# Expert results added to the tokens by one-hot products between the next pair's matrix products

## The chip, the cores and the metric

The kernel runs on one core of a Trainium2 chip. The metric is the device time of one execution in microseconds (us); lower is better. TensorE is called PE, VectorE DVE, ScalarE ACT, GpSimd POOL and SyncE SP, as in the profile.

## What is computed

Two transformer-like blocks over 512 tokens of width 1024, all in float32. The first (attention, recurrent branch, dense MLP) and the mixer of the second are not touched by the change. The change is in the last stage, a mixture of 64 experts of which each token uses two:

```python
y_pad = lax.map(expert_block, (x_pad..., block_e))   # silu(x@w_gate)*(x@w_up) @ w_down, per expert
y = y_pad[dest] * w_s[:, None]                       # weight of each of the 1024 (token, expert) rows
out = jax.ops.segment_sum(y, tok_s, num_segments=t)  # two rows to each token
```

`x + out` is then normalised and written. Each expert has three matrices of 2 MB (1024x512, 1024x512, 512x1024), so the stage reads 64 x 3 x 2 MB = 402.6 MB of weights, each once.

## The kernel before

The kernel has one hand-ordered program for each engine; semaphores carry the dependences. Experts are worked on two at a time, 32 pairs (`PAIRS`). Each expert has 64 places for tokens (`CAP`), so a pair's rows fill the 128 partitions; its two experts' products use 64 columns of the PE array each, side by side. (Tokens beyond 64 of one expert would go through the loop `more_rounds`, which these inputs do not enter.)

For pair q PE issues, in `pe_pair`: 8 transposes of the gathered token rows XG (tiles "xt", L992); gate and up products "g" and "u" (L1008, 8 k-steps x 2 experts each, N=512); 4 transposes of the activations ("at", L1015); the down products "d" in two halves (L1040; the last pair has its own order, L1028, that follows the weights as they land). A float32 product is two MATMUL records in the trace, so g and u are 64 records, d is 32. A tile is one of 8 PSUM banks, taken in turn by `any_bank`; `open_tile` waits until the bank's former tile was read.

Around it: DVE scales xt into XT (L2184), DVE and ACT turn g and u into AT (tanh L1423, DVE L2189 and L2194), ACT copies the transposes to aT (L1427), and DVE (L2204) and ACT (L1433) copy the halves of d into YE, the pair's 128 result rows. For pairs 0 to 30 POOL then scatters YE to a DRAM tensor `y_d` (L2321), a row for each (token, choice); the writers of YE wait for this of the pair before (`y_st`). POOL also gathers the token rows of pair q+2 into XG (L2317), queued behind the scatter of pair q-1 and ahead of that of pair q.

At the end eight gathers (L2317, `YA`, semaphores comb0 to comb7) fetch `y_d` back by token, and DVE adds each to X with its weight (`dve_comb`, L2126, eight instructions of 128x1024). Only pair 31 goes another way, `pe_spread` (L982): YE is scaled by the row's weight (`WTAB`, a small product "wtab", L961, behind pair 0), and multiplied by four one-hot matrices OH (128 rows x 128 tokens, made by `dve_hots`, L2140), one for each block of 128 tokens: 8 products of K=128, M=128, N=512, that is 16 records. `dve_spread` (L2133) adds these eight PSUM tiles to X. Then `act_end` (L1440, squares of each block), `dve_end` (root, L2210) and `sync_end` (output).

SP loads the weights, 192 loads of 2 MB into a ring of nine buffers (`RING`). Load n waits for the end of the products that used load n-9: each of g, u and d releases two buffers.

The lines of the writers of YE and of the PE loop:

```python
            if q:
                act.wait_ge(S("y_st"), 16 * q)                                   # L1430
...
                pe_pair(pe, T, q, ..., any_bank, ("gather", q % 2, 16 * ((q + 1) // 2)))   # L956
                if q == 0:                                                       # wtab, L957 to L962
...
            pe_spread(pe, PAIRS - 1, any_bank)                                   # L965
```

Of the kernel before, what the change touches and what calls it, by code (L numbers as in the profile page):

```python
# [16 lines left out]
PAIRS = 32  # L17
ENDS = 31
WIDE = 30
NONE = 4096  # L20
# [128 lines left out]
def program(nc, A, out):  # L149
    with ExitStack() as ctx:  # L150
# [160 lines left out]
        OK, o2 = zl(2, 4), zl(2, 4)  # L311
        V, WA, BW = zl(2, 4), zl(2, 4), zl(8, PAIRS - WIDE)
        GY = zl(2, 4).bitcast(I32)
        WTAB, TOKF = zl(PAIRS - WIDE), zl(PAIRS - WIDE)
        SLOTS, BM, BM0 = zl(128), zl(2, 4, 32), zl(2, 4)
# [18 lines left out]
        done_ck = SB[:, 4096 + CK_COLS["neg"][0]:4096 + CK_N + SM_N + 8 * 72 + 72 + 400]  # L334
        OH = [view(zone, 4096 + 512 * n, 4, 128) for n in range(3)]
        YA = [view(done_ck, 0, 1024), view(done_ck, 1024, 1024), view(zone, xt0 + 1024, 1024), row]
        YA += [view(EXTRA[0], 1024 * n, 1024) for n in range(4)]
        row2 = EXTRA[4][:, 0:1024]
# [24 lines left out]
        def slot(*name):  # L363
            return SLOT[W.at[name][0]]
# [12 lines left out]
        def tensor_program(pe):  # L377
# [575 lines left out]


            for q in range(PAIRS):
                pe_pair(pe, T, q, lambda n: loaded("ex", 6 * q + n), lambda n: slot("ex", 6 * q + n), any_bank, ("gather", q % 2, 16 * ((q + 1) // 2)))  # L956
                if q == 0:  # L957
                    o = open_tile(pe, ("wtab",), any_bank())
                    pe.wait_ge(S("bw"), 1)
                    for n in range(8):  # L960
                        ins = pe.matmul(o[:, 0:PAIRS - WIDE], AM[:, n // 4, n % 4, :], BW[:, n, :], start=n == 0, stop=n == 7)  # L961
                    ins.then_inc(T.f("wtab"), 1)  # L962
                for n in range(6):
                    W.ended[("ex", 6 * q + n)] = (("g", q), ("g", q), ("u", q), ("u", q), ("d", q, 1), ("d", q, 1))[n]
            pe_spread(pe, PAIRS - 1, any_bank)  # L965
            pe.wait_ge(S("rounds"), 1)

# [6 lines left out]

        def pe_spread(pe, q, bank):
            pe.wait_ge(S("oh"), 4)
            pe.wait_ge(*T.free("d", q, 0))
            pe.wait_ge(*T.free("d", q, 1))
            for i in range(4):
                for nh in range(2):  # L980
                    o = open_tile(pe, ("sp", q, i, nh), bank())
                    pe.matmul(o, OH[q - WIDE][:, i, :], YE[:, 512 * nh:512 * nh + 512], start=True, stop=True).then_inc(T.f("sp", q, i, nh), 1)  # L982

        def pe_pair(pe, table, q, ready, weight, bank, gathered):
            x = XT
# [8 lines left out]
            for mat, name in enumerate(("g", "u")):  # L994
                o = open_tile(pe, (name, q), bank(), 1, table)
                parts = mat == 1 and q == PAIRS - 1
                if not parts:
                    pe.wait_ge(*ready(2 * mat))
                    pe.wait_ge(*ready(2 * mat + 1))
                for k in range(8):  # L1000
                    if mat == 0 and k % 4 == 0:
                        pe.wait_ge(*table.free("xt", q, k // 4))
                    if parts and k == 0:
                        pe.wait_ge(S("up0"), 16)
                    if parts and k % 4 == 0:
                        pe.wait_ge(S(f"up{1 + k // 4}"), 16)
                    for e in range(2):
                        ins = pe.matmul(o[64 * e:64 * e + 64, :], x[:, k, 64 * e:64 * e + 64],  # L1008
                                        weight(2 * mat + e)[:, 512 * k:512 * k + 512], start=k == 0, stop=k == 7)
                ins.then_inc(table.f(name, q), 1)  # L1010
            o = open_tile(pe, ("at", q), bank(), 1, table)
            pe.wait_ge(*table.free("u", q))
            a = AT.rearrange("p (a b) -> p b a", b=4)
            for k in range(4):
                ins = pe.transpose(o[:, 128 * k:128 * k + 128], a[:, k, :], ident)  # L1015
            ins.then_inc(table.f("at", q), 1)
            pe.wait_ge(*table.free("at", q))
            if q == PAIRS - 1:
# [400 lines left out]
        def act_pair(act, table, q):  # L1419
# [9 lines left out]
            if q:  # L1429
                act.wait_ge(S("y_st"), 16 * q)  # L1430
            if q == ENDS:
                act.wait_ge(*table.free("wtab"))
            act.activation(YE[:, 512:1024], table.ap("d", q, 1), ACT.Copy,  # L1433
                           scale=WTAB[:, q - WIDE:q - WIDE + 1] if q >= ENDS else 1.0).then_inc(table.s("d", q, 1), 1)

# [11 lines left out]
        def vector_program(dve):  # L1447
# [623 lines left out]
            def weights():  # L2071
# [19 lines left out]
                flat8 = HI.rearrange("p a b -> p (a b)")  # L2091
                after(tt(BW, bc(iota[:, WIDE:PAIRS], 1, 8), bc(flat8, 2, PAIRS - WIDE), ALU.is_equal))
                dve.tensor_tensor(BW, BW, bc(WT.rearrange("p a b -> p (a b)"), 2, PAIRS - WIDE), ALU.mult).then_inc(S("bw"), 1)
                dve_rows(dve, own, ENDS)


            for q in range(ENDS):
                dve_pair(dve, T, q, weights if q == 0 else None)
                if q == 0:
                    copy(("wtab",), WTAB, T.ap("wtab")[:, 0:PAIRS - WIDE])  # L2100
                if q == 2:
                    dve_hots(dve, own)
            q = PAIRS - 1
            dve_xt(dve, T, q)
            dve_gate(dve, T, q)
            dve_up(dve, T, q)
            for i in range(2):
                dve_tokens(dve, i)
            dve_ye(dve, T, q)
            dve_tokens(dve, 2)  # L2110
            for i in range(2):
                dve_spread(dve, q, i)
            dve_tokens(dve, 3)
            for i in range(2, 4):
                dve_spread(dve, q, i)

        def dve_tokens(dve, i):
            for n in (2 * i, 2 * i + 1):
                dve_comb(dve, n, S("comb"), YA[n], S(f"comb{n}"))

# [6 lines left out]

        def dve_spread(dve, q, i):
            dve.wait_ge(S("comb"), 2 * i + 2)
            for nh in range(2):  # L2130
                xs = X[:, i, 512 * nh:512 * nh + 512]
                dve.wait_ge(*T.full("sp", q, i, nh))
                dve.tensor_tensor(xs, xs, T.ap("sp", q, i, nh), ALU.add).then_inc(S("xadd"), 1)  # L2133

        def dve_hots(dve, own):
            dve.wait_ge(*T.free("tab"))
            dve.wait_ge(own.sem, own(dve.tensor_copy(TOKF, TAB[:, WIDE:PAIRS])))
            for p in range(1, 2):
                for i in range(4):
                    dve.tensor_scalar(OH[p][:, i, :], ck("iota"), TOKF[:, p:p + 1], -128.0 * i, ALU.subtract, ALU.is_equal).then_inc(S("oh"), 1)  # L2140
        def dve_plan(dve, own, table):
# [28 lines left out]

        def dve_pair(dve, table, q, between=None):
            dve_xt(dve, table, q)
            if between:
                between()
            dve_gate(dve, table, q)
            dve_up(dve, table, q)
            dve_ye(dve, table, q)

# [17 lines left out]
        def dve_ye(dve, table, q):  # L2196
            dve.wait_ge(*table.full("d", q, 0))
            if q:
                dve.wait_ge(S("y_st"), 16 * q)
            if q >= ENDS:  # L2200
                dve.wait_ge(*table.free("wtab"))
                dve.tensor_scalar(YE[:, 0:512], table.ap("d", q, 0), WTAB[:, q - WIDE:q - WIDE + 1], None, ALU.mult).then_inc(table.s("d", q, 0), 1)
            else:
                dve.tensor_copy(YE[:, 0:512], table.ap("d", q, 0)).then_inc(table.s("d", q, 0), 1)  # L2204
# [25 lines left out]
        def gpsimd_program(pool):  # L2230
# [66 lines left out]
            for q in range(1, 3):  # L2297
                gather(pool, XG[q % 2], hn_d, TAB[:, q:q + 1], 511, S(f"gather{q % 2}"))
            for q in range(ENDS):
                if 0 < q < PAIRS - 2:  # L2300
                    pool.wait_ge(*T.full("xt", q, 1))
                    gather(pool, XG[q % 2], hn_d, TAB[:, q + 2:q + 3], 511, S(f"gather{q % 2}"))
                pool.wait_ge(*T.free("d", q, 0))
                pool.wait_ge(*T.free("d", q, 1))
                scatter(pool, DEST[:, q:q + 1], S("y_st"))


            pool.wait_ge(S("y_st"), 16 * ENDS)
            pool.wait_ge(S("gy"), 1)
            for n in range(8):  # L2310
                if n == 4:
                    pool.wait_ge(*T.full("u", PAIRS - 2))
                gather(pool, YA[n], y_d, GY[:, n % 2, n // 2:n // 2 + 1], 1023, S(f"comb{n}"))
            pool.wait_ge(S("xadd"), 8)
# [411 lines left out]
```

## Time and profile before

| what | us |
|---|---|
| median of three runs | 2460.68 (2452.25 to 2461.19) |
| the profiled execution | 2447.28 |
| its span, first to last instruction | 2445.4 |
| expert stage: first g product to last d product | 1469.3 to 2424.2 |
| rest: last pair's spread, sums, norm, output | 2424.2 to 2445.4 |

The profiled execution's own time lies 1.9 us above its span. Times in views count from the start of the span. A slice of the page's picture is 61 us; a digit is the busy share in tenths. In a timeline row the columns are start, duration, engine, line, operation, output and inputs, shapes, count, and in brackets the idle time of that engine just before and what ended it. "MATMUL ... 128*64" is an instruction on 64 columns of the array, "128*128" on all. The granted clock is 1.00 for 2.4 GHz and 0.5 for 1.2 GHz.

### The profile page before, as it was taken

To read this page: it belongs to the slowest core of one execution; us is meant where nothing else is said; L and a number is where in the kernel's file an instruction comes from. 1 tells how busy PE (TensorE), PEld (TensorE's weight loads), DVE (VectorE), ACT (ScalarE), POOL (GpSimd) and SP (SyncE) were. 2 spreads that over 40 slices of the span, in tenths; PEclk is the share of its full clock that TensorE was granted. 3 is DMA by queue.
4 is the path that set the end of the run, shared out by engine and by line. 5 is a ranking of instruction groups with operands and counts; after the bars stand their busy time and mean duration, and the time that the engine had idled before them with its cause. 6 is when DMAs were issued, how large, how long until landed. Compare 5 with 4: busy or idle time off the path is not lost.

```text
span 2445.4 us, 20383 instructions
## 1 busy us (share of the span) xinstructions
PE 2226.5 (91%) x8284; PEld 1022.6 (42%) x8284; DVE 612.2 (25%) x1311; ACT 323.1 (13%) x652; POOL 206.8 (8%) x186
## 2 busy tenths in 40 slices
PE   8999999999999999999999999988888888877886
PEld 4554444445444444466644463333323333322332
DVE  2246544311633210033431142111111111111114
ACT  2014424202111100021110120000000000000001
POOL 0001111010344200000000001000000000000001
PEclk9999999999999999998999999998999999999998
DMA  6201010322232321219422339999999999999995
GB/s 273 86 35 69 35 69 4 151 103 78 95 118 79 141 77 72 101 52 161 155 102 83 159 156 408 426 426 426 425 426 426 426 427 427 425 425 422 421 426 221
DMA packets 69759, 552.43 MB, mean 226 GB/s; under 512 B 21656, under 2 KB 26392, under 8 KB 37600
## 3 DMA queue, kind: packets, MB, share of 16 engines
q1 hardware_dynamic: 42384, 515.49, 51.8%
q10 hardware_dynamic: 17200, 23.23, 3.2%
q0 software_dynamic: 10080, 12.38, 1.4%
q8 instruction: 67, 1.10, 0.2%
q14 instruction: 28, 0.23, 0.0%
HBM read 543.91 MB, written 35.68 MB: 237 GB/s over the span
## 4 chain that ended last, share of the span: by engine, by line
PE 69%; DMA 26%; DVE 3%; ACT 1%; issue 1%; DVEq 0%; POOL 0%; SPq 0%; ACTq 0%; POOLq 0%
PE ps L380 25%; DMA sb<-in_eu 12%; PE ps L1008 9%; PE ps L456 8%; DMA sb<-in_eg 8%; PE ps L698 8%; PE ps L1040 4%; DMA sb<-in_ed 4%; PE ps L399 2%; PE ps L856 2%; PE ps L628 2%; PE ps L541 1%; PE ps L574 1%; PE ps L568 1%; DMA sb<-in_mgg 1%
## 5 line engine op out<-in xcount | busy, mean ns | idle before, releaser
L380 PE MATMUL ps<-sb 128*128 128x512 f32 (+2 forms) x1536 | 613.8, 559 | 2.8 <-issue 1.4
L1008 PE MATMUL ps<-sb 128*64 128x512 f32 x2048 | 487.7, 632 | 108.6 <-DMA sb<-in_eu 79.3
L380 PEld LDWEIGHTS ps<-sb 128*128 128x128 f32 x1536 | 279.7, 190 | 315.9 <-issue 312.6
L1008 PEld LDWEIGHTS ps<-sb 128*64 128x64 f32 x2048 | 176.7, 145 | 398.8 <-issue 398.7
L1040 PE MATMUL ps<-sb 128*64 128x512 f32 x992 | 232.5, 623 | 26.9 <-ACT sb L1427 17.2
L456 PE MATMUL ps<-sb 128*128 128x512 f32 x512 | 236.1, 600 | 0.3 <-DMA sb<-in_mgg 0.3
L698 PE MATMUL ps<-sb 128*128 128x512 f32 x448 | 192.5, 592 | 0.7 <-ACT sb L1247 0.7
L1451 DVE TENSOR_TENSOR sb<-sb 128x32 f32<-128x32 f32 (+10 forms) x292 | 115.4, 412 | 115.7 <-PE ps L662 66.2
L1040 PEld LDWEIGHTS ps<-sb 128*64 128x64 f32 x992 | 73.7, 143 | 164.2 <-issue 137.6
L456 PEld LDWEIGHTS ps<-sb 128*128 128x128 f32 x512 | 91.3, 190 | 100.0 <-issue 98.9
L698 PEld LDWEIGHTS ps<-sb 128*128 128x128 f32 x448 | 85.0, 190 | 107.6 <-issue 107.6
L2321 POOL DMA_INDIRECT y_d<-sb x31 | 31.2, 1007 | 853.1 <-PE ps L992 745.8
L2194 DVE SCALAR_TENSOR_TENSOR sb<-sb,ps 128x512 f32<-128x512 f32 x32 | 22.1, 690 | 300.8 <-PE ps L1008 294.2
L1070 ACT ACTIVATE sb<-ps 128x512 f32<-128x512 f32 (+4 forms) x103 | 54.6, 538 | 252.6 <-PE ps L380 90.9
L2189 DVE SCALAR_TENSOR_TENSOR sb<-sb,ps 128x512 f32<-128x512 f32 x32 | 22.1, 690 | 242.3 <-ACT sb L1423 242.3
L1475 DVE COPY sb<-ps 128x512 f32<-128x512 f32 (+6 forms) x53 | 34.5, 651 | 160.9 <-PE ps L380 89.8
L2239 POOL TENSOR_TENSOR sb<-sb 128x256 f32<-128x256 f32 (+3 forms) x32 | 41.6, 1300 | 377.4 <-DVE sb L1669 377.3
L1427 ACT ACTIVATE sb<-ps 128x512 f32<-128x512 f32 x32 | 19.1, 598 | 375.0 <-PE ps L1015 375.0
L2184 DVE TENSOR_TENSOR sb<-ps,sb 128x512 f32<-128x512 f32 x64 | 41.4, 688 | 101.8 <-PE ps L992 101.1
L2204 DVE COPY sb<-ps 128x512 f32<-128x512 f32 x31 | 21.5, 693 | 181.2 <-PE ps L1040 181.2
L399 PE MATMUL ps<-sb 128*128 128x256 f32 x256 | 59.6, 393 | 6.5 <-DVE sb L1470 3.5
L856 PE MATMUL ps<-sb 128*128 128x512 f32 x128 | 58.4, 598 | 1.6 <-DVE sb L1985 1.6
(283 smaller groups left out, 1481.5 us busy)
## 6 DMA issues: line engine op xcount, KB each, us to landing
sb<-in_eg SPq DMA_DIRECT2D x64, 2048.0 KB, 33.6
sb<-in_eu SPq DMA_DIRECT2D x63, 2048.0 KB, 33.9
sb<-in_ed SPq DMA_DIRECT2D x63, 2048.0 KB, 32.4
sb<-in_m SPq DMA_DIRECT2D x16, 2048.0 KB, 7.4
sb<-in_mg SPq DMA_DIRECT2D x8, 1536.0 KB, 6.9
sb<-in_winF SPq DMA_DIRECT2D x5, 2048.0 KB, 7.3
sb<-in_mgg SPq DMA_DIRECT2D x4, 2048.0 KB, 8.0
sb<-in_wo SPq DMA_DIRECT2D x4, 2048.0 KB, 7.3
```

The source lines that it names most:

```text
L380: ins = pe.matmul(out, lhsT, rhs, start=k == 0, stop=k == len(pieces) - 1)
L399: ins = pe.matmul(T.ap(*tile)[:, t], lhsT, rhs[:, t], start=k == 0, stop=k == 7)
L456: ins = pe.matmul(o, lhsT, rhs, start=k == 0, stop=k == 7)
L628: ins = pe.matmul(o, MG1[:, k, 128 * i:128 * i + 128], wo[nh][:, k, :], start=k == 0, stop=k == 7)
L698: ins = pe.matmul(acc[2 * i + nh], HT[:, k, 128 * i:128 * i + 128], w[:, q, 512 * nh:512 * nh + 512], start=k == 0, stop=False)
L856: ins = pe.matmul(T.ap(*name), MG2[:, k, 128 * i:128 * i + 128], wo[nh][:, k, :], start=k == 0, stop=k == 7)
L1008: ins = pe.matmul(o[64 * e:64 * e + 64, :], x[:, k, 64 * e:64 * e + 64], weight(2 * mat + e)[:, 512 * k:512 * k + 512], start=k == 0, stop ...
L1040: ins = pe.matmul(o[64 * e:64 * e + 64, :], aT[:, k, 64 * e:64 * e + 64], weight(4 + e)[:, d:d + 512], start=k == 0, stop=k == 3)
L1070: act.activation(dst, T.ap(*name) if src is None else src, ACT.Copy).then_inc(T.s(*name), 1)
L1451: return own(dve.tensor_tensor(o, a, b, op))
L2184: dve.tensor_tensor(XT[:, 4 * hf:4 * hf + 4, :], table.ap("xt", q, hf).rearrange("p (a b) -> p a b", a=4), bc(ck("gx")[:, 4 * hf:4 * hf + ...
L2239: pool.tensor_tensor(pr, pr, bc(ST[u % 4][:, 2:4], 2, nk), ALU.mult).then_inc(S("prob"), 1)
```

## The change

Every pair's result goes to the tokens by the way that only pair 31 had. The scatters, the eight gathers, `dve_comb` in the main path and the wait `y_st` are removed. All YE are scaled by the row's weight as they are copied (WTAB now has 32 columns). The products of pair q-1's YE with its one-hot matrices are issued inside pair q, in three places: the blocks 0 and 1 (4 products) between g and u, block 2 (2 products) between u and at, block 3 between at and d. Pair 31's come after it, as before. The writers of YE wait for the last of these products of the pair before. DVE makes four one-hot matrices for each pair and adds eight PSUM tiles to X for each. In pair 0 the product "wtab" moves from behind d to between u and at. POOL only gathers XG.

```diff
             for q in range(PAIRS):
-                pe_pair(...)
-                if q == 0:
-                    ... wtab ...
+                def meanwhile(place):
+                    if q:
+                        pe_spread(pe, q - 1, any_bank, ((0, 1), (2,), (3,))[place])
+                    elif place == 1:
+                        weight_table()
+                pe_pair(..., meanwhile)
-            pe_spread(pe, PAIRS - 1, any_bank)
+            pe_spread(pe, PAIRS - 1, any_bank, range(4))
...
+        def pe_spread(pe, q, bank, blocks):
+            if 0 in blocks:
+                pe.wait_ge(S("oh"), 4 * q + 4)
+                pe.wait_ge(*T.free("d", q, 0))
+                pe.wait_ge(*T.free("d", q, 1))
+            for i in blocks:
                 for nh in range(2):
                     o = open_tile(pe, ("sp", q, i, nh), bank())
+                    pe.matmul(o, OH[q % 2][:, i, :], YE[:, 512 * nh:512 * nh + 512], start=True, stop=True)...
...
                 ins.then_inc(table.f(name, q), 1)      # end of g (mat 0) and of u (mat 1)
+                if meanwhile:
+                    meanwhile(mat)
...
             ins.then_inc(table.f("at", q), 1)
+            if meanwhile:
+                meanwhile(2)
             pe.wait_ge(*table.free("at", q))
...
             if q:
-                act.wait_ge(S("y_st"), 16 * q)
+                act.wait_ge(*table.full("sp", q - 1, 3, 1))
...
+            for q in range(PAIRS):
+                def meanwhile(place):
+                    if q:
+                        dve_spread(dve, q - 1, ((0, 1), (2, 3))[place])
+                    if place == 0:
+                        if q == 0:
+                            weights()
+                            ... TOKF from TAB ...
+                        dve_hots(dve, q)
+                    elif q == 0:
+                        copy(("wtab",), WTAB, ...)
+                dve_pair(dve, T, q, meanwhile)
+            dve_spread(dve, PAIRS - 1, range(4))
...
             dve_gate(dve, table, q)
+            if meanwhile and q:
+                meanwhile(0)
             dve_up(dve, table, q)
+            if meanwhile:
+                meanwhile(1)
             dve_ye(dve, table, q)
...
-                pool.wait_ge(*T.free("d", q, 0))
-                pool.wait_ge(*T.free("d", q, 1))
-                scatter(pool, DEST[:, q:q + 1], S("y_st"))
-            pool.wait_ge(S("y_st"), 16 * ENDS)
-            pool.wait_ge(S("gy"), 1)
-            for n in range(8):
-                ...
-                gather(pool, YA[n], y_d, GY[:, n % 2, n // 2:n // 2 + 1], 1023, S(f"comb{n}"))
```

## Rows read from the trace of the kernel before

**Rows 1.** The page, part 2: busy tenths in 40 slices of 61 us.
```profile
PE   8999999999999999999999999988888888877886
...
DMA  6201010322232321219422339999999999999995
```

**Rows 2.** Windows: stretch, length, busy us (instructions) by engine, clock, DMA share, GB/s.
```profile
1547.53:1572.46 24.93, 22.79 (x109) 9.04 (x109) 3.37 (x6) 1.79 (x3) 2.03 (x3) 1.00 1.00 424
1944.03:1974.72 30.69, 24.70 (x109) 9.40 (x109) 3.36 (x5) 1.79 (x3) 2.02 (x2) 0.94 1.01 427
```

**Rows 3.** The chain that ended last, late in the expert stage: start, us, what.
```profile
2383.17 32.17 DMA sb<-in_ed
```

**Rows 4.** DMA queues, 1900 to 2200 us: packets, MB, share of 16 engines.
```profile
q1 hardware_dynamic: 8575, 124.92, 98.0%
q0 software_dynamic: 2880, 2.68, 2.6%
```

**Rows 5.** Timeline of pair 3, in which PE waits for no weights.
```profile
1547.53 13.96 PE L1008 MATMUL ps<-sb 128*64 128x512 f32 x64 [0.51 <-DVE sb L2184]
...
1562.43 0.72 PE L1015 MATMUL ps<-sb 128*128 128x128 f32 x4 [0.94 <-DVE sb L2194]
...
1563.84 7.09 PE L1040 MATMUL ps<-sb 128*64 128x512 f32 x32 [0.69 <-ACT sb L1427]
...
1572.46 13.95 PE L1008 MATMUL ps<-sb 128*64 128x512 f32 x64 [0.51 <-DVE sb L2184]
```

**Rows 6.** Timeline of a pair in mid-stage: the up products.
```profile
1944.03 8.78 PE L1008 MATMUL ps<-sb 128*64 128x512 f32 x32 [3.34 <-DMA sb<-in_eu]
...
1974.72 8.78 PE L1008 MATMUL ps<-sb 128*64 128x512 f32 x32 [3.40 <-DMA sb<-in_eu]
```

**Rows 7.** Timelines of single PE records where the tile shape changes.
```profile
1517.92 1.03 PE L1040 MATMUL ps<-sb 128*64 128x512 f32 x4
...
1518.77 0.60 PE L1040 MATMUL ps<-sb 128*64 128x512 f32 x2
1519.30 0.44 PE L992 MATMUL ps<-sb 128*128 128x128 f32 x2
...
1468.83 0.50 PE L950 MATMUL ps<-sb 128*128 128x64 f32 x3
1469.26 0.65 PE L1008 MATMUL ps<-sb 128*64 128x512 f32 x2
```

**Rows 8.** Timelines of single PE records: first and last of the spread products.
```profile
2425.15 0.67 PE L982 MATMUL ps<-sb 128*128 128x512 f32 x1 [0.98 <-ACT sb L1433]
...
2431.67 0.59 PE L982 MATMUL ps<-sb 128*128 128x512 f32 x1
```

**Rows 9.** Timeline: wtab, next transposes, and the making of four one-hot matrices.
```profile
1492.59 1.95 PE L961 MATMUL ps<-sb 128*128 128x2 f32 x16
...
1494.40 1.07 PE L992 MATMUL ps<-sb 128*128 128x128 f32 x8
...
1543.41 0.88 DVE L2140 TENSOR_SCALAR sb<-sb 128x128 f32<-128x128 f32 x4
```

**Rows 10.** Timeline: the down products of pair 2.
```profile
1537.21 8.79 PE L1040 MATMUL ps<-sb 128*64 128x512 f32 x32 [0.69 <-ACT sb L1427]
```

**Rows 11.** Timeline of the end: last d, spread, sums by DVE, last square.
```profile
2415.59 8.57 PE L1028 MATMUL ps<-sb 128*64 128x512 f32 x32 [3.19 <-DMA sb<-in_ed]
...
2425.15 7.11 PE L982 MATMUL ps<-sb 128*128 128x512 f32 x16 [0.98 <-ACT sb L1433]
...
2429.47 2.67 DVE L2126 SCALAR_TENSOR_TENSOR sb<-sb 128x1024 f32<-128x1024 f32 x2
...
2432.05 2.48 DVE L2133 TENSOR_TENSOR sb<-sb,ps 128x512 f32<-128x512 f32 x4
...
2434.56 1.06 ACT L1440 ACTIVATE sb<-sb 128x1024 f32<-128x1024 f32 x1
```

**Rows 12.** The page, part 6: the scatter's time to landing.
```profile
y_d<-sb POOLq DMA_INDIRECT x31, 10.2
```

## What the change should do to the time

> **What bounds the kernel now.** I read the page's picture first. Up to slice 24 PE is at 9 and DMA low; from there to the end of the expert stage DMA is at 9 and PE at 8 [rows 1]. So the stage that the change touches is the one place where the loads, not PE, set the time. The windows size it: a pair in mid-stage takes 30.69 us with DMA's share at 1.01, while a pair early in the stage, fed from buffers filled ahead, takes 24.93 us [rows 2]. What fills 30.69 us is 12.58 MB of weights. PE's wait is in plain sight: 3.34 us ahead of the up products, ended by a load, and these products then take 8.78 us [rows 6] where half of the 13.96 us of g and u, 7 us, would do [rows 5], because the granted clock fell in the wait (0.94 for the pair, [rows 2]). The chain agrees: its last long piece is a load that lands at 2415.3 [rows 3], after which only the last d products follow, to 2424.2 [rows 11].
>
> So PE has 30.69 - 24.93 = 5.8 us a pair to spare. The question is whether the added products fit.
>
> **What is removed.** For each pair one scatter, at the end eight gathers, and DVE's eight additions. The queue q0 took 2.6% of 300 us for ten scatters and ten gathers, 0.39 us each [rows 4]. Without the scatter the loads would need 30.3 us a pair, and the last weights would land 31 x 0.39 + 8 x 0.39 = 15 us earlier, at about 2400. That is all the gain DMA can give. The scatter's 10.2 us to landing [rows 12] was hidden: YE is written once in 25 to 31 us. POOL loses work and its gathers of XG start no later than before. The eight additions lie beside the last loads, except two, of 2.67 us, between the spread products and the last sums [rows 11].
>
> **What is added on PE.** Eight products of 128x512, 16 records, for pairs 0 to 30, each inside the next pair. The 16 of pair 31 are in the trace: the last starts 6.52 us after the first, so 0.43 us a record and 0.07 more for the first [rows 8]. 16 x 0.43 = 6.9 us is already more than the 5.8 us to spare, so it matters what of it goes into PE's holes, and what the changes of tile shape cost, for g, u and d run on 64 columns and the spread products on 128.
>
> A record lasts 0.60 us but the next starts 0.43 us after it (four records in two side-by-side pairs from 1517.92, the next two at 1518.77). From the last d records to the first transpose it is 0.53 us: a change from 64 to 128 columns costs 0.10 us. The other way, the last 64-element record of 128 columns starts at 1469.05 (0.50 us for three, the steps 0.11, the last lasting 0.28), the first g at 1469.26: 0.21 us, against 0.06 for 64 elements, so 0.15 us [rows 7]. Neither is seen between two long products; the bounds for a change are 0 (it hides; a gain is excluded, since the next record can't start before its step) and 0.35 us (the 0.17 us by which a record outlasts its step, and as much again to load the next weights), and I take 0.10 and 0.15, since all 31 changes behind d show the one.
>
> Pair by pair, against the 24.93 us:
> - between g and u, where there is no hole: 8 x 0.43 + 0.07 + 0.10 + 0.15 = 3.8 us;
> - between u and at: 4 x 0.43 + 0.07 + 0.10 = 1.9 us, into a hole of 0.94 us and the 0.17 us in which the last record only finishes [rows 5]: 0.8 us remain;
> - between at and d: 4 x 0.43 + 0.15 = 1.9 us, into 0.69 us and 0.16 us: 1.0 us remains;
> - the 0.51 us between transposes and g stays.
>
> Together 5.5 us, so PE needs 24.93 + 5.5 = 30.4 us a pair, with no weights to wait for and the clock at 1.00. With changes of shape free it is 29.9; with 0.35 us each, in four places, 31.3.
>
> **A rule that bears on it.** The change from d to the transposes costs 0.10 us, less than the 0.17 us in which the last records finish [rows 7]. The Trainium skill, TensorEngine Tiling (Array Packing), Key Properties, says that changing the tiling mode (not just the tile) drains TensorE. The trace agrees that a change isn't free, though not that the whole of a record's tail is waited for; a full drain at each of the four would make 0.17 us of each 0.10 to 0.15 us, which adds 0.2 us a pair.
>
> **Which ends last.** Loads need 30.3 us a pair, PE 30.4. The two are close, but not in place: by the end of the early pairs loads are ahead of need. With PE at 30.4 us the last weights land at about 2400 and the last d products begin near 2430, so PE is last throughout, by up to 27 us. The ring doesn't turn this round: g, u and d each free two buffers, some 10 us apart, in which two loads of 4.9 us (a sixth of 30.3 less the gather) run, and what is loaded is needed a pair later.
>
> Pair 0: wtab takes 1.95 us behind d [rows 9]; put into the hole of 1.1 us between u and at it costs 0.9, so the transposes of pair 1 start not at 1494.4 but at about 1493.5. From there 31 pairs of 30.4 (30.43 before rounding) end the last d at 1493.5 + 943.3 = 2436.8, which is 12.6 us later than 2424.2 [rows 11].
>
> The end: YE, the spread of pair 31, sums, squares are the same. Without the two additions in between, the last sum follows its product: the product ends at 2431.67 + 0.59 = 2432.26 [rows 8], the sum 0.7 later at 2433.0, where now DVE ends at 2432.05 + 2.48 = 2434.5 and the last square starts [rows 11]. That gives 1.5 us.
>
> Sum: 12.6 - 1.5 = 11.1 us. On the profiled execution's 2447.28 us that is 2458.4.
>
> **What else is added, at nothing.** DVE gets eight sums of 0.62 to 0.69 us (2.48 us for four, [rows 11]) and four one-hot matrices in 0.88 us [rows 9], 6.4 us on 3.37 [rows 2]: 9.8 of 30.4 us. Queued behind them on DVE are the up step, which PE awaits, and the copy of d. The sums of blocks 0 and 1 and the one-hots end some 5 us after g, and u ends 10 us after g; those of blocks 2 and 3 end while d runs. PSUM: a tile opens on the bank of the eighth before it; for the first half of d that is the first tile of block 1, summed long before. The wait of YE's writers is for products that PE issues ahead of d, so it is met. If DVE lost this cover, each us would be paid 31 times.
>
> **The median.** The runs' median, 2460.68, lies 13.4 us above the profiled execution, and nothing shown says where. If it is slower loading, the changed kernel, bound by PE, doesn't have it, and comes at 2458; if it is elsewhere, it comes at 2472. I take the middle but one: 2467, which is 0.25% above the median. About 0.5% (12 us) is what a measurement of this kernel can tell from no change.
>
> **The rivals.**
> - *Slower: the changes of shape cost more between long products.* Place: four in each of 31 pairs. For it: both kinds seen cost something, and never between two 512-element products. Against it: the one seen 31 times is 0.10. At 0.35 us each a pair takes 31.3 us, the end 28 us later, 2486 to 2500. It decides (over 0.5% slower) from 0.01 us a change above mine if the median's offset stays, from 0.12 us if not.
> - *Slower: the clock falls in the hole that is left.* In pair 2, with no wait for weights, d took 8.79 us, not 7.09, just behind the holes on both sides of at [rows 10]. The change fills these; left are the transposes and 0.51 us before g. If that still costs 1.7 us in two pairs of five, it is 21 us: 2480 to 2490. Against it: in none of the pairs before the loads became the bound was g slow behind that hole (13.95 and 13.96, [rows 5]).
> - *Faster: PE keeps within the loads.* If the added products cost PE 5 us a pair or less (changes free, holes filled to the last), PE ends by 1493.5 + 31 x 29.9 = 2420; with still less, the loads' own end decides, 15 us earlier than now. With the 1.5 us at the end that is 2447.3 - 5.3 = 2442 to 2431 against the profiled execution, up to 13 us more against the median: 2431 to 2455, most of it near 2444. For it: PE's holes are real, 5.8 us. Against it: 6.9 us is counted from records of the very product.
> - That the change doesn't remove what it says is not a rival: the eight gathers and scatters are gone in the code. But they were hidden, which is why the forecast has no gain from them.
>
> **How the numbers follow.** Forecast (PE at 30.2 to 30.6 us a pair): 0.5. Dearer changes of shape 0.2, the clock 0.15, loads the bound 0.15. The forecast's own range, with both readings of the median, is 2450 to 2477. Leaving out the ends of both sides, the range is 2446 to 2488. Part of the forecast lies above 0.5%, part of the slower rivals below it: faster 0.13, same 0.5, slower 0.37.
>
> **What would show it.** In the profile after: PE at 9 in the slices from 24, DMA a little under its full share; in mid-stage 30.4 us from one g to the next, with no idle time ended by in_eg, in_eu or in_ed; 0.53 us from the last g record to the first spread record; clock 1.00 there; the last load landed 20 us and more before its products; the last d near 2437. The forecast is wrong if PE still waits for loads, if up products take over 7.1 us, or if a wait on DVE stands before at or d.

## The result: slightly slower, and bound by PE

Over 20 runs of each kernel the median is 2460.3 us with the change and 2452.2 us before; the ratio is 1.0029, 95% interval 1.0016 to 1.0041 (the two medians alone give 1.0033). That is a slowdown of 0.3%, small but clear of noise. The forecast was 2467 us, 0.25% over the median of the three runs known then.

The profiled execution of the changed kernel has a span of 2459.9 us. The page's picture (part 2, slices of 61 us) answers to [rows 1]: PE now stays at 9 through the expert stage, and so does its granted clock.

```profile
PE   8999999999999999999999999999999999999997
...
PEclk9999999999999999998999999999999999999999
DMA  6201110321232321219422349999999999999992
```

DMA's digit is 9 as before, so it can't tell which of the two sets the time. These lines can: a window over one pair in mid-stage (columns as in [rows 2]), and the page's part 6, where the last figure is the us from issue to landing.

```profile
1955.27:1985.67 30.40, 29.89 (x125) 11.30 (x125) 9.62 (x18) 1.89 (x3) 0.98 (x1) 1.00 1.00 415
...
sb<-in_eg SPq DMA_DIRECT2D x64, 2048.0 KB, 14.3
sb<-in_eu SPq DMA_DIRECT2D x63, 2048.0 KB, 12.7
sb<-in_ed SPq DMA_DIRECT2D x63, 2048.0 KB, 11.4
```

The same rows of the page of before:

```profile
sb<-in_eg SPq DMA_DIRECT2D x64, 2048.0 KB, 33.6
sb<-in_eu SPq DMA_DIRECT2D x63, 2048.0 KB, 33.9
sb<-in_ed SPq DMA_DIRECT2D x63, 2048.0 KB, 32.4
```

PE is busy for 29.89 of 30.40 us, at a clock of 1.00; before it was 24.70 of 30.69 at 0.94 [rows 2]. A load takes 11 to 14 us from issue to landing, where it took 32 to 34 us before: fewer loads stand in front of it, because buffers now come free more slowly than DMA could fill them (the last experiment has a kernel in which DMA fills them faster). The last weights are there at 2406.3 us, 27 us before their products begin at 2433.05. The groups of PE instructions in the stage agree, by what ended the idle time before them (the last column). Not one wait is ended by a load:

```profile
L1015 PE MATMUL ps<-sb 128*64 128x512 f32 x1982 | 439.0, 595 | 15.3 <-DVE sb L2190 15.3
L989 PE MATMUL ps<-sb 128*128 128x512 f32 x496 | 234.8, 605 | 0.0
L1051 PE MATMUL ps<-sb 128*64 128x512 f32 x960 | 212.6, 595 | 0.0
```

(L1015 is g and u, L989 the one-hot products, L1051 d, L999 the transposes xt, L1024 at, L2135 the sums into X. In the kernels of the experiments these lines stand a few numbers off.) The timeline of one pair shows where the products stand. Between them PE stops for 0.51 us only, behind the transposes; from one g to the next it is 1955.27 - 1924.87 = 30.40 us.

```profile
1924.87 7.09 PE L1015 MATMUL ps<-sb 128*64 128x512 f32 x32 [0.51 <-DVE sb L2190]
...
1931.89 3.71 PE L989 MATMUL ps<-sb 128*128 128x512 f32 x8
...
1935.52 7.09 PE L1015 MATMUL ps<-sb 128*64 128x512 f32 x32
...
1942.54 1.99 PE L989 MATMUL ps<-sb 128*128 128x512 f32 x4
...
1944.37 0.63 PE L1024 MATMUL ps<-sb 128*128 128x128 f32 x4
...
1944.83 1.88 PE L989 MATMUL ps<-sb 128*128 128x512 f32 x4
...
1946.65 7.09 PE L1051 MATMUL ps<-sb 128*64 128x512 f32 x32
...
1955.27 7.09 PE L1015 MATMUL ps<-sb 128*64 128x512 f32 x32 [0.51 <-DVE sb L2190]
```

By parts the two profiled executions compare so:

| part | before | after |
|---|---|---|
| start to first g | 1469.3 | 1473.6 |
| first g to end of last d | 954.9 | 966.6 |
| end of last d to end | 21.3 | 19.8 |

The stage is 11.7 us longer, the end 1.5 us shorter. The first part, which the change doesn't touch, is 4.3 us longer. That is chance: in the nine profiled executions with the change or a variant of it the first g starts at 1469.3 us on average, the same as before. So 10.2 us of the 14.5 between the two spans are the change's.

### The profile page after: what moved, and what is told of

Same layout as the page of the kernel before. It is cut to its first block, busy times and chain, and to the rows that moved or that the text cites. A ratio compares the mean times of both kernels' runs of the same rounds, so it can differ in the third digit from the quotient of the medians.

```text
span 2459.9 us, 21919 instructions
## 1 busy us (share of the span) xinstructions
PE 2395.5 (97%) x8780; PEld 1084.6 (44%) x8780; DVE 795.1 (32%) x1665; ACT 326.0 (13%) x652; POOL 166.7 (7%) x147
## 4 chain that ended last, share of the span: by engine, by line
PE 94%; DVE 3%; DMA 2%; ACT 1%; issue 1%; DVEq 0%; POOL 0%; SPq 0%; ACTq 0%; POOLq 0%
PE ps L377 25%; PE ps L1015 18%; PE ps L989 9%; PE ps L1051 9%; PE ps L453 8%; PE ps L695 8%; PE ps L396 2%; PE ps L853 2%; PE ps L625 2%; PE ps L538 1%; DVE sb L2190 1%; PE ps L571 1%; PE ps L565 1%; PE ps L999 1%; DMA sb<-in_mgg 1%
## 5 line engine op out<-in xcount | busy, mean ns | idle before, releaser
L1015 PE MATMUL ps<-sb 128*64 128x512 f32 x2048 | 453.4, 595 | 15.8 <-DVE sb L2190 15.8
L377 PEld LDWEIGHTS ps<-sb 128*128 128x128 f32 x1536 | 279.7, 190 | 316.2 <-issue 312.9
L1015 PEld LDWEIGHTS ps<-sb 128*64 128x64 f32 x2048 | 155.3, 137 | 289.4 <-issue 289.3
L989 PE MATMUL ps<-sb 128*128 128x512 f32 x512 | 241.9, 605 | 1.0 <-ACT sb L1444 1.0
L453 PE MATMUL ps<-sb 128*128 128x512 f32 x512 | 238.1, 604 | 0.3 <-DMA sb<-in_mgg 0.3
L1051 PE MATMUL ps<-sb 128*64 128x512 f32 x992 | 219.7, 595 | 0.7 <-ACT sb L1438 0.7
L695 PE MATMUL ps<-sb 128*128 128x512 f32 x448 | 192.5, 592 | 0.7 <-ACT sb L1258 0.7
L2135 DVE TENSOR_TENSOR sb<-sb,ps 128x512 f32<-128x512 f32 x256 | 175.8, 687 | 53.6 <-PE ps L989 53.6
L989 PEld LDWEIGHTS ps<-sb 128*128 128x128 f32 x512 | 89.9, 190 | 130.0 <-issue 130.0
L453 PEld LDWEIGHTS ps<-sb 128*128 128x128 f32 x512 | 92.1, 191 | 101.1 <-issue 100.0
L1051 PEld LDWEIGHTS ps<-sb 128*64 128x64 f32 x992 | 68.5, 137 | 147.5 <-issue 146.7
L695 PEld LDWEIGHTS ps<-sb 128*128 128x128 f32 x448 | 85.0, 190 | 107.6 <-issue 107.6
L2312 POOL DMA_INDIRECT sb<-hn_d,sb x31 | 30.7, 991 | 930.1 <-PE ps L999 846.4
```

Of the source, the lines that this page charges most:

```text
L377: ins = pe.matmul(out, lhsT, rhs, start=k == 0, stop=k == len(pieces) - 1)
L453: ins = pe.matmul(o, lhsT, rhs, start=k == 0, stop=k == 7)
L695: ins = pe.matmul(acc[2 * i + nh], HT[:, k, 128 * i:128 * i + 128], w[:, q, 512 * nh:512 * nh + 512], start=k == 0, stop=False)
L989: pe.matmul(o, OH[q % 2][:, i, :], YE[:, 512 * nh:512 * nh + 512], start=True, stop=True).then_inc(T.f("sp", q, i, nh), 1)
L1051: ins = pe.matmul(o[64 * e:64 * e + 64, :], aT[:, k, 64 * e:64 * e + 64], weight(4 + e)[:, d:d + 512], start=k == 0, stop=k == 3)
```

## Experiments

The theory: with the change a pair costs what PE's own steps add up to, and loads, DVE and POOL are beside the path. Rivals: loads still set a part; DVE's longer queue delays PE; changes of tile shape drain the array; the clock falls in the holes. All kernels are the changed kernel with one edit. Each was timed beside the kernel before on the same chip; "a pair" is the time from one g to the next in the profile.

**Loads alone.** The products of pairs 0 to 30 are left out.

```diff
-                    if q:
-                        pe_spread(pe, q - 1, any_bank, ((0, 1), (2,), (3,))[place])
-                    elif place == 1:
+                    if q == 0 and place == 1:
                         weight_table()
```

> The changed kernel without the one-hot products of pairs 0 to 30 and without their sums into X (their results are left out; only pair 31's reach the tokens); the scatters and gathers are gone as well. It shows what the loads alone need. Theory: 30.3 us a pair in mid-stage against 30.7 before, last weights near 2400, in all 15 us less than before, 0.6 to 0.7% faster. Rival 1 (a scatter costs the loads nothing): 30.7 a pair, equal to before. Rival 2 (scatters disturb the loads by more than their own time): 29.9 or less a pair, 25 us or more less.

Measured: ratio 0.991 (0.988 to 0.993). In mid-stage (from pair 10 to pair 25, by the starts of g) a pair takes 30.2 us, against 30.8 before. The timeline again shows up products that wait for loads, and the clock's price for it (8.78 us and 8.63 us instead of 7.09):

```profile
1897.79 7.09 PE L1013 MATMUL ps<-sb 128*64 128x512 f32 x32 [0.51 <-DVE sb L2182]
1909.62 8.63 PE L1013 MATMUL ps<-sb 128*64 128x512 f32 x32 [4.74 <-DMA sb<-in_eu]
1929.31 7.09 PE L1013 MATMUL ps<-sb 128*64 128x512 f32 x32 [0.59 <-DVE sb L2182]
1939.05 8.78 PE L1013 MATMUL ps<-sb 128*64 128x512 f32 x32 [2.66 <-DMA sb<-in_eu]
```

The first g to the end of the last d (1472.85 to 2405.16) is 932.3 us, 22.6 less than before. Of these, 1.0 us isn't traffic but `wtab`'s move in pair 0 (25.71 us from its g to the next, 26.72 before). That leaves 21.6 us where 15 were expected, between the theory and the second rival: the pair is as expected, the sum is larger by some 6 us. So the removed DRAM traffic is worth some 20 us, 0.8%, when PE has room; the rest of the 0.9% is `wtab` and the 1.5 us of the end. Part of the 6 us lies late in the stage, where the page of before shows 422 and 421 GB/s against 425 and more in most slices earlier, and this kernel 426 to 428; why the kernel before is slower there was not settled.

**Scatters kept.** The changed kernel, with POOL still scattering each YE to DRAM.

```diff
+                pool.wait_ge(*T.free("d", q, 0))
+                pool.wait_ge(*T.free("d", q, 1))
+                scatter(pool, DEST[:, q:q + 1], S("y_st"))
```

> The changed kernel with the 31 scatters to DRAM kept as well (nothing reads them back; YE's writers wait for them too). Theory (PE is the bound, loads 0.1 us below it): loads now need 30.7 us a pair against PE's 30.4, but run ahead of need by over 20 us, so at most some us are added; equal to the changed kernel within 5 us, 0.2 to 0.5% slower than before. Rival (the changed kernel is bound by loads too): 12 us or more slower than the changed kernel, 0.8% slower than before.

Measured: ratio 1.0049 (1.0029 to 1.0068), median 2462.0, within 2 us of the changed kernel. A pair takes 30.40 us, to the hundredth what it takes without them:

```profile
1892.07 7.09 PE L1015 MATMUL ps<-sb 128*64 128x512 f32 x32 [0.51 <-DVE sb L2192]
...
1922.47 7.09 PE L1015 MATMUL ps<-sb 128*64 128x512 f32 x32 [0.51 <-DVE sb L2192]
```

From the first g to the end of the last d both kernels take 966.6 us. With the products in place the scatters are worth nothing: loads are off the path. (The eight gathers at the end were not put back. This run says nothing of them.)

**Nothing in PE's holes.** All eight products between g and u.

```diff
-                        pe_spread(pe, q - 1, any_bank, ((0, 1), (2,), (3,))[place])
+                        pe_spread(pe, q - 1, any_bank, ((0, 1, 2, 3), (), (), ())[place])
```

(A fourth place, behind the transposes xt, stays empty here and in the kernel with blocks 0 to 2 behind u. DVE's sums move along with the products.)

> The changed kernel with all eight products between g and u and none in the holes around at. Theory (a pair's time is the sum of PE's steps): 16 steps of 0.43 us, 0.10 for the first and two changes of shape of 0.09 us stand in full: 24.93 + 7.2 = 32.1 us a pair, 1.7 us more than with the change, 53 us more in all. If the two holes that the change fills are worth nothing (something else, such as the loads or DVE, sets the pair's time), it is equal to the changed kernel.

Measured: ratio 1.037 (1.033 to 1.042), median 2533.8 over four runs, 73 us over the changed kernel where 53 were expected. In 18 of the 30 pairs from pair 1 on, a pair takes 32.16 us, the 32.1 of the sum. In the other 12 it takes 33.85, and the timeline shows where the 1.70 us are:

```profile
1907.28 0.72 PE L1026 MATMUL ps<-sb 128*128 128x128 f32 x4 [0.95 <-DVE sb L2204]
1908.69 8.78 PE L1053 MATMUL ps<-sb 128*64 128x512 f32 x32 [0.69 <-ACT sb L1440]
1917.40 1.09 PE L999 MATMUL ps<-sb 128*128 128x128 f32 x8
1919.00 7.09 PE L1017 MATMUL ps<-sb 128*64 128x512 f32 x32 [0.51 <-DVE sb L2194]
```

Behind the two open holes around at (0.95 and 0.69 us) d takes 8.78 us, as in pair 2 before the change [rows 10]. The window over these products has a mean granted clock of 0.80, so it stood at the lower level (0.5) for a part of them:

```profile
1908.69:1917.40 8.71, 8.71 (x32) 2.60 (x33) 0.75 (x1) 0.00 (x0) 0.00 (x0) 0.80 0.99 421
```

12 x 1.70 = 20 us is the rest. So the holes' filling is worth 1.75 us a pair in the steps and, on average, 0.7 more in the clock. Why 12 of the 30 pairs and not the others was not settled. In the changed kernel, where only the hole of the transposes is left, it happens in none of the 32 pairs.

**Two more changes of tile shape.** Block 0's products moved into the middle of g.

```diff
                 for k in range(8):
+                    if mat == 0 and k == 4 and meanwhile:
+                        meanwhile(3)
```

(with `((1,), (2,), (3,), (0,))[place]`)

> The changed kernel, but block 0's products stand in the middle of g (after four of its eight k-steps) and block 1's behind it: two changes of tile shape more in each pair, nothing else. Theory from the changed kernel's trace (0.09 us for each change, 0.10 more for the first spread product, 0.05 more for the first of g): 0.3 us a pair, so 30.7 us, 10 us more in all. Rival (a change drains the array, 0.17 us and a load of weights each): 0.7 us a pair or more, 22 us in all. Rival (a change is hidden): nothing.

Measured: ratio 1.011 (1.008 to 1.014). A pair takes 30.75 us, 0.35 more than with the change, all 30 pairs alike; over 31 pairs 11 us. (The two medians differ by 13 us.) The timeline shows the cut g:

```profile
1901.46 3.65 PE L1017 MATMUL ps<-sb 128*64 128x512 f32 x16 [0.51 <-DVE sb L2192]
1905.04 1.99 PE L989 MATMUL ps<-sb 128*128 128x512 f32 x4
1906.96 3.65 PE L1017 MATMUL ps<-sb 128*64 128x512 f32 x16
...
1932.20 2.37 PE L1017 MATMUL ps<-sb 128*64 128x512 f32 x10 [0.51 <-DVE sb L2192]
```

A pair of changes costs 0.35 us with the first records' extra in it: neither nothing nor the 0.7 of the rival.

**More work on DVE.** Four, and then ten, more copies ahead of each pair's one-hot matrices.

```diff
         def dve_hots(dve, q):
+            for n in range(4):       # 10 in the second kernel
+                if 4 * q + n:
+                    dve.wait_ge(S("extra"), 4 * q + n)
+                dve.tensor_copy(view(done_ck, 1344, 1024), row).then_inc(S("extra"), 1)
```

> The changed kernel with four more DVE copies of 128x1024 (of a row to a scratch row, one after another) ahead of each pair's one-hot matrices. DVE idles 5.6 us between the one-hot matrices and the up step in the changed kernel's trace. Theory (DVE's work is covered): if four take less than that together, 30.40 us a pair, the same as the changed kernel. Rival (DVE's queue already delays PE): each us added costs a us, 31 times.

Measured: ratio 1.0035 (1.0016 to 1.0053), a pair takes 30.40 us; four copies take 2.87 us of DVE's idle time.

> As the run with four more copies on DVE, with ten. Theory: of what the ten take together, 5.6 us are DVE's idle time and 0.8 us PE's slack behind block 2's products; what is beyond 6.4 us is added to each pair. At 1.1 us a copy that is 4.6 us a pair (35.0), at 0.65 us it is 0.1 (30.5).

Measured: ratio 1.013 (1.010 to 1.017), over two runs. Ten copies take 7.24 us, 0.84 over the 6.4; a pair takes 1930.23 - 1899.11 = 31.12 us, 0.72 more. PE now waits for the up step ahead of at:

```profile
1910.48 7.24 DVE L2143 COPY sb<-sb 128x1024 f32<-128x1024 f32 x10
...
1919.24 0.72 PE L1024 MATMUL ps<-sb 128*128 128x128 f32 x4 [0.47 <-DVE sb L2204]
```

DVE's cover is real, and its length is nearly as read: 7.24 - 0.72 = 6.5 us a pair, where 6.4 was read.

**Other places for the products.** First blocks 0 to 2 between u and at, block 3 behind at:

```diff
-                        pe_spread(pe, q - 1, any_bank, ((0, 1), (2,), (3,))[place])
+                        pe_spread(pe, q - 1, any_bank, ((), (0, 1, 2), (3,), ())[place])
```

> The changed kernel, but blocks 0, 1 and 2 stand between u and at, block 3 between at and d: two changes of tile shape fewer in a pair, and nothing between g and u. Theory (PE is the bound): PE needs 24.9 + 4.2 + 1.0 = 30.1 us a pair, 0.3 less than with the change, just under or at the loads' 30.3; 3 to 10 us faster than the changed kernel, about equal to the kernel before. Rival (loads or DVE set the time): the same as the changed kernel, 0.3% slower than before.

Measured: ratio 1.0007 (0.999 to 1.0024), no difference from before; a pair takes 30.05 us (1881.24, 1911.29, 1941.34). That is 0.35 less than with the change: g and u run on without a change of shape between them.

Then the place behind the transposes xt is used, so that the last hole is filled too:

```diff
+                if meanwhile:
+                    meanwhile(3)                     # behind the eight transposes xt
...
+                        pe_spread(pe, q - 1, any_bank, ((), (1, 2), (3,), (0,))[place])
```

(DVE sums block 0 behind its two xt steps.)

> The changed kernel, but block 0's two products stand between the transposes xt and g (filling that hole), blocks 1 and 2 between u and at, block 3 between at and d, none between g and u. Theory (PE is the bound after the change, loads just below): PE needs 24.9 + 1.2 + 2.5 + 1.0 = 29.6 us a pair, less than the 30.3 us that the loads should need without scatters, so the loads become the bound again and the profiled stage ends 13 to 18 us earlier than before the change: about 0.6% faster than the kernel before. Rival (loads or DVE already set the changed kernel's time): no gain over the changed kernel, about 0.3% slower than before.

Measured: ratio 0.996 (0.994 to 0.998), median 2438.7. This is the fastest complete kernel, 0.4% faster than before. Against the changed kernel it is 0.7% faster by the two ratios and 0.9% by the two medians; 31 x 0.73 us, the difference of a pair, is 0.9%. A pair takes 29.67 us and g follows without a wait:

```profile
1905.72 1.29 DVE L2194 TENSOR_TENSOR sb<-ps,sb 128x512 f32<-128x512 f32 x2 [3.33 <-PE ps L999]
1906.01 1.96 PE L989 MATMUL ps<-sb 128*128 128x512 f32 x4
...
1907.90 13.95 PE L1017 MATMUL ps<-sb 128*64 128x512 f32 x64
...
1937.57 13.96 PE L1017 MATMUL ps<-sb 128*64 128x512 f32 x64
```

The pair is as the theory had it (29.6); that the loads would bind again was wrong. An up load takes 16 us from issue to landing at the start of the stage and 26 us at its end (`--dma`, windows 1500:1700 and 2200:2400):

```profile
sb<-in_eu SPq DMA_DIRECT2D x13, 2048.0 KB, 16.4
...
sb<-in_eu SPq DMA_DIRECT2D x11, 2048.0 KB, 25.8
```

The landings in the trace say the same: g's second load lands 21 us ahead of g in pair 2 and 10 us ahead in pair 30. The loads lose 0.4 us a pair, so they need 30.1 us where PE takes 29.67, yet PE never waited for one: 31 pairs are too few to use the lead up. The expected gain (0.6%) was read from the loads' end. PE's own sum ends later: by the prediction's way of counting, 1493.5 + 31 x 29.67 = 2413.3, 10.9 us ahead of before, and from the first g to the end of the last d it is 944.1 us, 10.8 less. The kernel without products has the longer pair in mid-stage (30.2) and the shorter stage (932.3), because its early pairs, whose weights are there, take 25 to 27 us each; here they take 29.67 like all others. Its median, 2427.3, shows that 11 us are left for whoever makes PE shorter.

## Why the forecast came out as it did

- **PE becomes the bound, at 30.4 us a pair:** right, measured 30.40 in all 30 pairs. Term by term, from the timelines of [rows 5] and of the pair above: between g and u 3.8 expected, 3.78 measured (10.65 us from start to start, 6.87 before); between u and at 0.8 expected, 0.82 measured (8.85 against 8.03); between at and d 1.0 expected, 0.87 measured (2.28 against 1.41); from d to the next g nothing, and 8.62 us in both. The prediction adds its three parts up to 5.5 us, but they are 3.8 + 0.8 + 1.0 = 5.6 (5.56 before rounding), which would have made 1.9 us more over 31 pairs; measured are 5.47. So a slip hid part of an error. The error is mostly at's four records, which take 0.63 us with products in front of them and 0.72 us behind a hole.
- **Changes of shape:** from 64 to 128 columns 0.10 expected. From 128 to 64 0.15 was taken from a short product; between long ones it is 0.09, as these single records show (start, us):

```profile
1931.33 0.63 PE L1015 MATMUL ps<-sb 128*64 128x512 f32 x2
1931.89 0.70 PE L989 MATMUL ps<-sb 128*128 128x512 f32 x1
...
1935.00 0.59 PE L989 MATMUL ps<-sb 128*128 128x512 f32 x1
1935.52 0.65 PE L1015 MATMUL ps<-sb 128*64 128x512 f32 x2
```

  The last two g records start 0.56 and 0.52 us ahead of the first spread product, the last spread product 0.52 ahead of u; in steady flow it is 0.43. Over the two changes of a pair the 0.15 is 0.12 us too large. The first spread product's extra, 0.10 rather than 0.07 in two places, and 0.05 for the first record of u, which the sum left out, give nearly all of it back. A full drain, as the Trainium skill (TensorEngine Tiling (Array Packing), Key Properties) has it for a change of tiling mode, isn't what the trace shows: the next record starts 0.07 us before the one ahead of it has ended (by the ends in the profile, which are modelled).
- **Removed DRAM traffic gives nothing:** right; keeping the scatters changes no pair. Its worth to the loads if PE had room was put at 15 us (0.39 us a transfer) and is 21.6.
- **DVE, PSUM, POOL, the new wait of YE's writers:** at nothing, right; the two runs with more DVE work give the cover's end.
- **The end:** 1.5 us shorter expected and measured (21.3 to 19.8). The sums follow their products, one by one:

```profile
2441.12 7.11 PE L989 MATMUL ps<-sb 128*128 128x512 f32 x16 [0.99 <-ACT sb L1444]
...
2448.28 0.69 DVE L2135 TENSOR_TENSOR sb<-sb,ps 128x512 f32<-128x512 f32 x1 [0.17 <-PE ps L989]
2449.00 1.06 ACT L1450 ACTIVATE sb<-sb 128x1024 f32<-128x1024 f32 x1 [0.57 <-DVE sb L2135]
```

- **The sum:** 11.1 us expected, 10.2 in the profiled stage and end, 8.1 between the medians.
- **The step that failed is the last one, from the sum to the call.** The sum says 11.1 us more, 0.45%, out of 31 equal pairs; the call was "same" (0.5, against 0.37 for slower), because "about 0.5% (12 us) is what a measurement of this kernel can tell from no change". That doesn't hold. Over 20 runs of each kernel the ratio's interval is 1.0016 to 1.0041, some 3 us to either side, and the 8.1 us by which the medians differ are clear of it. No row stood behind the 12 us; they are near the spread of single runs (2446 to 2461 before), which a median of 20 narrows. A sum like this should have been called a small slowdown.
- **The step from the profile to the median failed with it.** The 13.4 us between the profiled execution and the median of three runs were taken for something that the change might or might not remove, and 8.6 of them were added to 2458.4 to make 2467. Over 20 runs the median of before is 2452.2: two of the three runs had been among its slowest. So 8.5 of the 13.4 us were sampling. The forecast was 6.7 us high, and its ratio came out as 1.0025 where the sum said 1.0045. That 1.0025 lies so near the measured 1.0029 is luck, and so is the profiled sum's 2458.4, within 2 us of 2460.3: it starts from an execution 4.9 us below the median and adds 3.0 us too much.
- **Rivals:** dearer changes of shape, refuted. The clock, refuted for the change, but real: with the holes open it costs 20 us. The loads as bound, refuted; the fastest place that was tried is still bound by PE.

## What to carry to other kernels

When work is moved from DMA to PE, set what it costs PE beside PE's spare time in each period, record by record: here 6.9 us of products against 5.8 us of room. Where the added work stands matters as much as its size; with the same eight products a pair took 29.7, 30.1, 30.4, 30.75 or at least 32.2 us by where they were put, best in the holes that PE has anyway and next to work of the same tile shape. And a lead that one resource has at the start of a stage can cover its slower rate to the end: compare when things are needed, not only rates. Last, an effect that repeats in every period is small but sure: count how many runs it takes to see it before calling it nothing.

## What was not expected

- The part before the stage isn't the same from run to run: in the ten profiled executions, whose programs do the same work up to there, the first g starts between 1463.2 and 1476.1 us. They come apart in the first 200 us and between 1050 and 1200 us, by some us each time; in between they run alike to 0.1 us. That is the size of the effect asked for; comparing the stage alone, from g to the end, takes it out. What makes these differences was not studied.
- In the changed kernel, with PE as the bound, the stage is periodic to 0.01 us; with loads as the bound a pair takes 27.0 to 33.0 us (the kernel without products).
- DMA's share reads 1.00 both where loads bound the kernel and where they don't. The time from issue to landing tells them apart: 33 us against 13.
